# Attention weights turned as three pieces of one 352-column row in a two-layer encoder kernel

## The reference

```python
s_meta = einsum('bnqhgd,bmhd->bnhgqm', qf, k_meta) * scale
s_band = einsum('bnqhgd,bnkhd->bnhgqk', qf, k_band) * scale
s_band = where(visible, s_band, -inf)
p = softmax(concatenate([s_meta, s_band, sink], axis=-1), axis=-1)
p_meta, p_band = p[..., :16], p[..., 16:144]
o_frames = (einsum('bnhgqm,bmhd->bnqhgd', p_meta, v_meta)
            + einsum('bnhgqk,bnkhd->bnqhgd', p_band, v_band))
return o @ w_out
```

## Time and profile before

| what | value |
|---|---|
| median of 3 runs | 1044.42 us (1042.7 to 1046.78) |
| the profiled execution's own time | 1043.23 us |
| its span | 1041.4 us |
| TensorE busy | 1028.1 us (99% of the span) |
| VectorE, ScalarE busy | 643.1 us, 519.4 us |
| the second layer's mixer | about 772 to 846 us of the span |

### The profile page before, as it was taken

One profiled execution on the slowest core, in us unless ns is written; L12 is line 12 of the kernel. 1 busy time (PEld: TensorE's weight loads), 2 busy tenths in 40 slices (PEclk: granted clock), 3 DMA queues, 4 the chain that ended last, 5 costly groups with the idle time before them and its releaser, 6 DMA issues.

```text
span 1041.4 us, 19994 instructions
## 1 busy us (share of the span) xinstructions
PE 1028.1 (99%) x8070; PEld 997.1 (96%) x8070; DVE 643.1 (62%) x896; ACT 519.4 (50%) x742; POOL 10.5 (1%) x19
## 2 busy tenths in 40 slices
PE   9999999999999999999999999999999999999997
PEld 8999999999999999999999999999998999999886
DVE  5765554478775875554447755543589777765533
ACT  5653353446675564434345634443457756544433
POOL 0000000000000000000000000000021000000000
PEclk9999999999999999999999999999999999999999
DMA  8564554514333266455542655455413335655551
GB/s 326 203 242 161 178 186 162 177 66 145 140 127 117 82 213 224 168 165 182 179 166 77 243 178 184 162 171 192 162 41 123 114 131 202 218 185 191 173 182 40
DMA packets 24533, 171.26 MB, mean 164 GB/s; under 512 B 2976, under 2 KB 2976, under 8 KB 4384
## 3 DMA queue, kind: packets, MB, share of 16 engines
q1 hardware_dynamic: 24048, 169.49, 46.7%
q10 hardware_dynamic: 432, 1.00, 0.2%
HBM read 169.43 MB, written 1.05 MB: 164 GB/s over the span
## 4 chain that ended last, share of the span: by engine, by line
PE 92%; DVE 3%; ACT 2%; DMA 2%; issue 1%; DVEq 0%; SPq 0%; ACTq 0%
PE ps L1156 24%; PE ps L1158 24%; PE ps L1157 24%; PE ps L1192 3%; PE ps L1201 2%; PE ps L1194 2%; PE ps L1494 2%; PE ps L1495 2%; PE ps L1493 2%; DMA raw<-in_panels_dram 1%; PE ps L1260 1%; ACT w_hi L517 1%; PE ps L1315 1%; PE ps L1400 1%; DMA first<-in_first_dram 1%; PE ps L1415 1%
## 5 line engine op out<-in xcount | busy, mean ns | idle before, releaser
L517 ACT CAST w_hi<-raw 128x1024 fp32r<-128x1024 f32 x312 | 312.5, 1047 | 398.3 <-PE ps L1158 301.8
L767 DVE TENSOR_TENSOR w_lo<-raw,w_hi 128x1024 fp32r<-128x1024 f32 x312 | 369.9, 1225 | 188.6 <-ACT w_hi L517 188.2
L1156 PE MATMUL ps<-y_hi,w_lo 128*128 128x272 f32 (+1 forms) x1458 | 422.1, 290 | 0.4 <-DVE w_lo L767 0.2
L1158 PE MATMUL ps<-y_lo,w_hi 128*128 128x272 f32 (+1 forms) x1458 | 419.0, 287 | 0.0
L1157 PE MATMUL ps<-y_hi,w_hi 128*128 128x272 f32 (+1 forms) x1458 | 417.4, 286 | 0.0
L1156 PEld LDWEIGHTS ps<-y_hi,w_lo 128*128 128x128 f32 x1458 | 274.7, 188 | 2.4 <-issue 1.5
L1157 PEld LDWEIGHTS ps<-y_hi,w_hi 128*128 128x128 f32 x1458 | 274.6, 188 | 0.2
L1158 PEld LDWEIGHTS ps<-y_lo,w_hi 128*128 128x128 f32 x1458 | 274.7, 188 | 0.0
L1156 PE MATMUL ps<-h_hi,w_lo 128*128 (+1 forms) x528 | 152.1, 288 | 0.0
L1157 PE MATMUL ps<-h_hi,w_hi 128*128 (+1 forms) x528 | 152.1, 288 | 0.0
L1158 PE MATMUL ps<-h_lo,w_hi 128*128 (+1 forms) x528 | 151.3, 287 | 0.0
(11 more groups left out here) (173 smaller groups left out, 1033.9 us busy)
## 6 DMA issues: line engine op xcount, KB each, us to landing
raw<-in_panels_dram SPq DMA_DIRECT2D x156, 1024.0 KB, 4.9
first<-in_first_dram SPq DMA_DIRECT2D x3, 784.0 KB, 8.1
xT<-in_x_dram SPq DMA_DIRECT2D x1, 1088.0 KB, 14.4
out_dram<-fT SPq DMA_DIRECT2D x4, 256.0 KB, 2.0
const<-in_const_dram ACTq DMA_DIRECT2D x1, 920.0 KB, 9.9
first<-in_first_dram SPq DMA_DIRECT2D x2, 392.0 KB, 3.9
gain_row<-in_row_dram SPq DMA_DIRECT2D x1, 512.0 KB, 5.7
gains<-in_gains_dram ACTq DMA_DIRECT2D x1, 48.0 KB, 3.8
```

Of the source, the lines that this page charges most:

```text
L517: nc.scalar.copy(w_hi[:, g % SLOTS, part], raw_part(g, part)).then_inc(hi_ready, 1)
L767: nc.vector.tensor_tensor(w_lo[:, g % SLOTS, part], raw_part(g, part), w_hi[:, g % SLOTS, part].bitcast(F32), ALU.subtract).then_inc(lo_re ...
L1156: nc.tensor.matmul(dst, w_lo[:, slot, pc], yh, start=first, stop=False, skip_group_check=shared)
L1158: return nc.tensor.matmul(dst, w_hi[:, slot, pc], yl, start=False, stop=last, skip_group_check=shared)
```

## The change

The row of 352 columns is cut without overlap into three pieces of 128, 128 and 96 columns (`SW_TILE`). Each head's weights are turned in three transposes, not four, and ScalarE copies 384 columns, not 512. The middle piece holds the last 16 keys of block 0 and the first 112 of block 1. `values` still makes four products for each head: block 0 with piece 0 (128 keys) and with the first 16 partitions of piece 1; block 1 with all 128 partitions of piece 1, where the 16 that belong to block 0 meet zeros in `v_win`, and with the 96 partitions of piece 2. GpSimd fills `v_win` with 8 instructions in place of 7, and `turn_v` waits for 8.

```diff
-SW_WIN = [(0, 0, 0), (0, 16, 112), (1, 0, 0), (1, 80, 48)]
+SW_TILE = [(0, P), (P, P), (2 * P, SW_W - 2 * P)]
+SW_WIN = [(0, 0), (0, 1), (1, 1), (1, 2)]
+def window(n):
+    c, tile = SW_WIN[n]
+    at, width = SW_TILE[tile]
+    lo, hi = max(at, SW_COL[c]), min(at + width, SW_COL[c] + SW_KEYS[c])
+    return lo - at, hi - at, SW_TOKENS[c][lo - SW_COL[c]:hi - SW_COL[c]]
...
-            p_t = swa_sb("p_t", [P, 2, 2, 512])
+            p_t = swa_sb("p_t", [P, 2, 2, len(SW_TILE) * P])
...
-                    for n, (c, k0, zero) in enumerate(SW_WIN):
+                    for n in range(4):
+                        zero, end, tokens = window(n)
                         if zero:
                             nc.gpsimd.memset(v_win[:, :, n, 0:zero], 0.0).then_inc(win_ready, 1)
-                        tokens = SW_TOKENS[c][k0 + zero:k0 + P]
+                        if end < P:
+                            nc.gpsimd.memset(v_win[:, :, n, end:P], 0.0).then_inc(win_ready, 1)
...
-                            nc.scalar.copy(p_t[:, p % 2, half], ps[:, 2 + half, :]).then_inc(pt_saved, 1)
+                            nc.scalar.copy(p_t[:, p % 2, half], ps[:, 2 + half, 0:len(SW_TILE) * P]).then_inc(pt_saved, 1)
...
-                            for n, (c, k0, _) in enumerate(SW_WIN):
-                                at = SW_COL[c] + k0
-                                mm = nc.tensor.transpose(ps[:, 2 + half, P * n:P * n + P],
-                                                         s[:, p % 3, half, at:at + P], cst("ident"))
+                            for n, (at, width) in enumerate(SW_TILE):
+                                mm = nc.tensor.transpose(ps[0:width, 2 + half, P * n:P * n + P],
+                                                         s[:, p % 3, half, at:at + width], cst("ident"))
...
-                        for n, (c, _, zero) in enumerate(SW_WIN):
+                        for n, (c, tile) in enumerate(SW_WIN):
+                            keys = window(n)[1]
                             for half in range(2):
                                 r = slice(HD * half, HD * half + HD)
-                                mm = nc.tensor.matmul(ps[r, 4, P * c:P * c + P], vt[:, n, vc],
-                                                      p_t[:, p % 2, half, P * n:P * n + P], start=(zero == 0),
-                                                      stop=(zero > 0), skip_group_check=True)
+                                mm = nc.tensor.matmul(ps[r, 4, P * c:P * c + P], vt[0:keys, n, vc],
+                                                      p_t[0:keys, p % 2, half, P * tile:P * tile + P],
+                                                      start=(n % 2 == 0), stop=(n % 2 == 1), skip_group_check=True)
...
-                        pe.wait_ge(win_ready, 7)
+                        pe.wait_ge(win_ready, 8)
```

## The result

The changed kernel took 1045.46 us in the median of 15 runs (1043.03 to 1048.59), the kernel before 1042.70 us in 15 runs beside them (1042.25 to 1046.78): ratio 1.0022, 95% interval 1.0015 to 1.0029. That is 2.3 us slower by the ratio and 2.8 by the medians, within the 0.5% called no change, but clear of the scatter. I had reasoned +0.5 us, on a base of 1043.8 us, the middle of four executions, which was 1.1 us too high.

What follows compares the result with a forecast made beforehand. TensorE was taken as the bound, busy 1028.1 of 1041.4 us. Cut changes +2.56 and transposes -1.74 gave +0.8 us on it; the stage's end slips 0.3 to 0.8, taken +0.5: 1043.8 + 0.5 = 1044.3 us, range 1041.1 to 1047.3.

Steps and rivals of the forecast that it cites:

- Turns: Weight transposes on TensorE: 16 fewer at 0.109 us each, 1.74 us off; 96-column ones priced like the others.
- case D: Rival: the 96-column transposes take two records each, +2.3 us with the copies' share off; chance 0.03.
- Changes of cut: Value products on TensorE: 16 new switches of array tiling around the 16-key products, 0.16 us each, +2.56 us (0 to 5.2).
- Case B: Rival: the 16-key value product costs no change of the array's cut, so the kernel gains, -1.9 us; chance 0.22.
- case C: Rival: the 16-key products' records run alone and pay unoverlapped latency plus both cut changes, +9.4 us; chance 0.03.
- the mark: Value group's time in the chain: forecast about 1.3 us; growth past 1.6 us would show the prediction wrong.
- The sign that I had named: Test for changes of cut: the 16-key products' records would show another tile in their row, 32 rows or 64.
- TensorE's sum: TensorE's net work in the stage: 2.56 us of cut changes less 1.74 us of transposes, +0.8 us.
- The slip of the chain: Chain up to its exit in pair 6's turn: +1.92 cut changes, -1.42 transposes, -0.22 ScalarE copies, giving +0.3 us.
- The transfer: Panel transfer near the stage's end, on the chain to the sums: 4.88 us, with no change of duration forecast.
- TensorE is nearly as late: Stage end: TensorE's last output unit, which ScalarE awaited 0.29 us, slips +0.8 us; the sums need it too.
- The base: Starting time for the forecast: 1043.8 us, the middle of the profiled execution and three runs together.

Runs made afterwards that it cites:

- e7: Changed kernel, with each output unit waiting for its second pair of heads only ahead of the first matmul reading it; ratio 0.9997 to the kernel before.
- e12: Changed kernel plus 8 useless transposes in TensorE's wait ahead of the mixer, to shift the instruction fetch; ratio 1.0009 to the kernel before.
- e4: Changed kernel plus 16 useless transposes in TensorE's wait ahead of the mixer, restoring later instructions' addresses; ratio 1.0010 to the kernel before.
- e13: Changed kernel with the 16-key product run over 64 partitions, zeros beyond 16; profiled only: value group 1.33 us, stage 69.5 us.
- e3: Changed kernel with the 16-key product first of the four, so one new change of cut per pair; ratio 1.0003 to the kernel before.
- e8: Changed kernel with ScalarE's end of the mixer reordered: first x tile scaled before the last casts, first squares before the fT copies; ratio 1.0001 to the kernel before.
- e2: Changed kernel with the 16-key product run over all 128 partitions of piece 1, zeros included; ratio 0.9980 to the kernel before.
- e14: Changed kernel with the 16-key product run over 96 partitions; profiled only: value group 1.03 us, stage 68.1 us.
- e15_before_2: Kernel before, unaltered, second of three more profiles; profiled only: last critical transfer 7.3 us, stage 71.0 us.
- e10: Kernel before (four windows) with the later output-unit wait and the reordered ScalarE tail; ratio 0.9997 to the kernel before.
- e11: Changed kernel unaltered, measured again as a control on another chip; ratio 1.0005 to the kernel before.
- e1: Changed kernel unaltered, run once for a second profile; last critical transfer 5.4 us, stage 70.1 us.

## Why the prediction was wrong

**Turns: right.** 16 x 0.109 us was forecast. A turn of six records takes 0.65 us (0.87 for eight), 0.80 right behind value products (1.02): 0.22 us for two transposes, 0.11 each. The 96-column ones cost the same as the others and are one record; case D fell.

**Changes of cut: right, and their size too.** 0.16 us was taken, 0.15 measured, at zero, one and two changes. Case B fell with the group at 1.32 us and the 0.17 us of idle time in the load queue around `16*64`; case C with the same 1.32 us, where 1.6 was the mark. The sign that I had named, another tile in the row, was a poor one: `96*64` has it too and cost nothing.

**TensorE's sum: a term was missing.** "TensorE in sum: +0.8 us" holds for its own work (8 x 0.30 - 8 x 0.22 = 0.64). I had named what ends the waits of ScalarE, but not looked for what the longer turns covered on TensorE: the way from the value group over `sw_hi` and `sw_lo` to the output units of slots 6 and 8. The turn lay over it. When it shrank, 0.33 us of wait came up (e7).

**The slip of the chain: the step that failed first.** I let the chain go on leaving TensorE in pair 6's turn over ScalarE's copies, and took their 0.22 us off. But in the kernel before, ScalarE's `sw_hi` of pair 6 started at 830.08, when TensorE's products for it were just finished, at 829.95 (TensorE in order of time, kernel before):

```profile
828.86 1.09 PE L1427 MATMUL ps<-p_t,vt 128*64 128x128 f32 x16
```

A second path ran right beside, and it got longer while the first got shorter. By it the issue slips by seven pairs of value group and turn (7 x 0.08 = 0.56) and 0.33 of waits, 0.9 us; measured 0.91 in the first two profiles and 0.95 between the medians of all ten, forecast +0.3.

**The transfer: taken for a constant.** The 4.88 us of the earlier trace rows went into the sum as they were. In the changed kernel it is 6.2 to 6.4 us in most profiles, and the stage ends 6.2 us after its landing. This is the larger part of the stage's growth in the profiles (1.4 of 2.4 us). "TensorE is nearly as late" did not come up in the changed kernel's profile, since the chain over the transfer slipped more; with an early transfer it does, but by way of the slot of weights and not of the last squares (e12).

**The base.** 1043.8 us from four executions; 15 gave 1042.7. The 1.1 us too much stood in for a part of the loss that the sum left out, so 1044.3 lies nearer to 1045.46 than the sum deserves; that is luck.

**Why the transfer is late, and what stays open.** It goes with the fetches of instructions on queue q8. (That they are TensorE's is not named in the trace; e4 and e12, where more TensorE instructions moved them, suggest it.) Of 300 panel transfers issued from 40 us on in the first two profiles, eight took over 5.9 us; of the 236 without a q8 packet within 0.5 us of the time from issue to landing none took over 5.2. The packet that falls into the changed kernel's late transfer starts at 837.70 us (view of the queues from 837.6 to 837.8 us) and by its share of that view (29.6% of 16 engines over 0.2 us) it takes 0.95 us, to 838.65:

```profile
q8 instruction: 1, 0.02, 29.6%
```

By 837.7 all but one of the transfer's own packets are through; from 837.75 to 838.6 none starts. One is left, and it starts as the fetch ends (from 838.6 to 838.7 us; the transfer lands at 839.70):

```profile
q1 hardware_dynamic: 1, 0.00, 1.6%
```

In e13 the fetch comes at the same time of the stage, but no packet of the transfer is left behind it (from 838.05 to 839.2 us), and the transfer took 4.8 us:

```profile
DMA packets 0, 0.00 MB, mean 0 GB/s; under 512 B 0, under 2 KB 0, under 8 KB 0
```

This holds for all eleven profiles in which the fetch started 3.6 to 4.6 us behind the issue. In the eight late ones (the changed kernel's five, e3, e7, e8) a packet of the transfer starts within 0.02 us of the fetch's end; in the three early ones (e2, e13, e14) none does. So in these profiles what makes the transfer late is a piece of it that stands behind the fetch. The trace does not name the DMA engine of a packet; that both were on one is read from the times.

Three things stay open. In e15_before_2 and e10 the fetch comes at the start of the transfer (0.6 and 0.5 us behind the issue), as in the early profiles of the kernel before, and yet the transfer is late. A fetch is also not the only cause: the transfer issued at 841.9 us in the kernel before, one of the eight, took 6.3 us with the packet starting only at its landing, and in e11 one issued at 333.2 us took 7.0 us with none near. And why the fetch falls where it does is not shown: it comes at 58.0 to 58.1 us of the stage in all four profiles of the kernel before and at 62.6 to 62.8 in the five late ones of the changed kernel, but at 59.5 in e1, the same program. That removing 32 instructions moved it into the transfer is argued; e12 speaks for it in the profile and against it in the time.

## What to carry to other kernels

Before products are made smaller, look whether their rows of the array stay in the cut of their neighbours: here 96 rows were free, and 64 or 16 between products of 128 cost 0.15 us at each edge, more than the transposes saved; zeros over all 128 rows were the better bargain (e2). When a group of instructions gets shorter, ask what ran in its shadow on the same engine's behalf. And where the chain leaves the bound engine, look for the path right beside it and don't enter a transfer's duration from a single profile as a constant.

## What the runs showed of the hardware

With 64 held columns a change of cut costs 0.15 us (e3, one change) and a pair 0.30 us, equal for 16 and for 64 rows (1.32 and 1.33 us against 1.03 for 96 and 128). In the group with a pair the load queue stands idle for 0.17 us at each change. A transpose with 96 held columns costs what one with 128 does: 0.11 us. In the first two profiles, from 40 us on, panels of 1 MB landed in at most 5.2 us when no instruction packet was near, and in up to 6.6 us with one (7.3 in e15_before_2). The instruction packet in the changed kernel's late transfer took 0.95 us, and a transfer of which a packet started at such a packet's end landed in 6.1 to 6.6 us in eight profiles, where 4.7 to 4.9 were usual. In the stage, the same program's q8 packet appears at different times, 59.5 us in e1 and 62.6 to 62.8 in the other five profiles, though the issue of the transfer beside it stands at 58.4 to 58.6 us in all.
